# Row and token scales spread over partitions: from products with ones to a round trip through DRAM

## The reference, cut to what matters

```
def rms_norm(x, g):
    xf = x.astype(jnp.float32)
    y = xf * lax.rsqrt(jnp.mean(xf * xf, axis=-1, keepdims=True) + EPS)
    return (y * g.astype(jnp.float32)).astype(x.dtype)
...
        ple_gate = jax.nn.sigmoid(jnp.einsum('bsd,de->bse', rms_norm(x, norm_ple_g[i]), w_ple_gate[i]))
        x = x + ple_gate * jnp.einsum('bsq,qd->bsd', p[i], w_ple_proj[i])
    return rms_norm(x, norm_final_g)
...
    def step(carry, inp):
        C, n, m = carry
        C_l, n_l, am, gc = inp
        m_new = jnp.maximum(gc + m, am)
        sp = jnp.exp(gc + m - m_new)
        sl = jnp.exp(am - m_new)
        C_new = sp[..., None, None] * C + sl[..., None, None] * C_l
```

## Time and profile before

| What | Value |
|---|---|
| median of three runs | 1969.47 us |
| the profiled execution, as timed | 1970.42 us |
| its span in the profile | 1968.6 us |
| PE busy | 1884.6 us (96%) |
| VectorE busy | 729.1 us (37%) |
| ScalarE busy | 516.8 us (26%) |
| mean DMA rate over the span | 257 GB/s |
| mean granted TensorE clock | 0.989 |

### The profile page before, as it was taken

One profiled execution on the slowest core, in us unless ns is written; L12 is line 12 of the kernel. 1 busy time (PEld: TensorE's weight loads), 2 busy tenths in 40 slices (PEclk: granted clock), 3 DMA queues, 4 the chain that ended last, 5 costly groups with the idle time before them and its releaser, 6 DMA issues.

```text
span 1968.6 us, 20653 instructions
## 1 busy us (share of the span) xinstructions
PE 1884.6 (96%) x8719; PEld 1146.5 (58%) x8719; DVE 729.1 (37%) x1216; ACT 516.8 (26%) x836; POOL 58.6 (3%) x58
## 2 busy tenths in 40 slices
PE   8999999999999999999997999999889998999898
PEld 6788888888887888877874333333333332333332
DVE  7544444333356765886453111111111110111112
ACT  5444323222245343276622000000000000000002
POOL 1000000000014001000010000000000000000000
PEclk9999999999999999999998999999999999999999
DMA  5221322322323234212387999999999999999997
GB/s 190 86 86 65 118 96 97 97 97 96 107 95 107 75 112 161 75 65 78 141 328 292 430 432 434 430 432 433 433 432 434 430 433 433 431 433 433 431 429 294
DMA packets 50476, 506.89 MB, mean 257 GB/s; under 512 B 6544, under 2 KB 7568, under 8 KB 31696
## 3 DMA queue, kind: packets, MB, share of 16 engines
q1 hardware_dynamic: 48288, 502.22, 62.3%
q10 hardware_dynamic: 2096, 3.35, 0.5%
HBM read 501.23 MB, written 4.33 MB: 257 GB/s over the span
## 4 chain that ended last, share of the span: by engine, by line
PE 73%; DMA 23%; DVE 2%; ACT 2%; issue 1%; ACTq 0%; SPq 0%; DVEq 0%
PE ps L2133 40%; DMA ring_a<-in_experts_in 23%; PE ps L2484 10%; PE ps L2495 7%; PE ps L2068 4%; PE ps L2443 2%; PE ps L2467 1%; PE ps L2305 1%; PE ps L2530 1%; PE ps L2282 1%; PE ps L2506 0%; ACT hidT L1255 0%; PE ps L2183 0%; PE ps L2180 0%; PE ps L2186 0%
## 5 line engine op out<-in xcount | busy, mean ns | idle before, releaser
L2484 PE MATMUL ps<-ring_a,xe 128*64 128x512 f32 x1504 | 343.8, 610 | 41.9 <-DMA ring_a<-in_experts_in 41.1
L2484 PEld LDWEIGHTS ps<-ring_a,xe 128*64 128x64 f32 x1504 | 107.0, 140 | 272.8 <-issue 211.4
L1300 DVE TENSOR_TENSOR d_lo<-d_raw,d_hi 128x1024 fp32r<-128x1024 f32 x166 | 204.4, 1240 | 118.9 <-ACT d_hi L850 118.2
L2133 PE MATMUL ps<-n_hi,d_hi 128*128 128x512 f32 x448 | 176.0, 393 | 1.5 <-DVE d_lo L1300 0.8
L2133 PE MATMUL ps<-n_lo,d_hi 128*128 128x512 f32 x448 | 174.5, 389 | 0.0
L2133 PE MATMUL ps<-n_hi,d_lo 128*128 128x512 f32 x448 | 174.3, 389 | 0.0
L850 ACT ACTIVATE d_hi<-d_raw 128x1024 fp32r<-128x1024 f32 x166 | 170.8, 1049 | 8.6 <-DMA d_raw<-in_tiles_in 6.9
L1530 DVE TENSOR_TENSOR hid<-hid,ps 128x512 f32<-128x512 f32 x32 | 20.7, 684 | 409.1 <-PE ps L2484 382.7
L1976 DVE TENSOR_TENSOR acc<-acc,ps 128x1024 f32<-128x1024 f32 x56 | 64.6, 1215 | 244.5 <-PE ps L2467 244.5
L2495 PE MATMUL ps<-ring_a,hidT 128*64 128x512 f32 x648 | 145.9, 596 | 8.7 <-DMA ring_a<-in_experts_in 5.5
L2484 PE MATMUL ps<-ring_b,xe 128*64 128x512 f32 x464 | 103.1, 593 | 1.6 <-DMA ring_b<-in_experts_in 1.6
(11 more groups left out here) (499 smaller groups left out, 2710.6 us busy)
## 6 DMA issues: line engine op xcount, KB each, us to landing
ring_a<-in_experts_in SPq DMA_DIRECT2D x56, 4096.0 KB, 41.8
ring_b<-in_experts_in SPq DMA_DIRECT2D x28, 3072.0 KB, 42.7
d_raw<-in_tiles_in SPq DMA_DIRECT2D x166, 512.0 KB, 3.3
ring_a<-in_experts_in SPq DMA_DIRECT2D x31, 1024.0 KB, 12.4
ring_a<-in_experts_in SPq DMA_DIRECT2D x12, 2048.0 KB, 13.4
ring_b<-in_experts_in SPq DMA_DIRECT2D x5, 2048.0 KB, 13.2
ring_b<-in_experts_in SPq DMA_DIRECT2D x8, 1024.0 KB, 16.6
x_in<-in_xT_in SPq DMA_DIRECT2D x4, 512.0 KB, 6.7
```

The costliest lines, as they stand in the source:

```text
L1300: dve.tensor_tensor(d_lo[:, n % SLOTS, :, :], d_raw[:, n % SLOTS, :, :], d_hi[:, n % SLOTS, :, :].bitcast(F32), ALU.subtract).then_inc(t_l ...
L2133: mm = pe.matmul(bank, lt[:, n, gr.k0 + k, :], rt[:, k, :], start=k == 0 and m == 0, stop=k == gr.nk - 1 and m == 2)
L2484: mm = pe.matmul(ps[half * CAP:(half + 1) * CAP, 2 * m + q, :], xe[:, k, :], slot(e, n)[:, (2 * q + half) * S:(2 * q + half + 1) * S], sta ...
```

## The change

The four products, the three diagonals of 128 x 512, the one of 64 x 256, the three VectorE copies and the one ScalarE copy go away. In their place the 128 x 4 scales are stored in DRAM, element by element, and loaded back as a row to all partitions. The first two stores and loads stand in SP's queue in front of the load of a tile, and SP waits for the reciprocal and for its own store; VectorE waits for the load. The router's scale is stored together with dq's and loaded at out2 0. The chunk decays (64 x 4) go through ScalarE's queue, beside the row maxima.

```diff
+            def first_after(name, i):
+                return min(n for n in range(SLOTS, len(TILES)) if LAST[n - SLOTS] >= AT[name, i])
...
                     if STREAM[FIRST[n]].i == 0:
                         sp.wait_ge(do_lo.sem, do_lo.count("lo", NH - 1))
+                        sp.wait_ge(d_q.sem, d_q.count("root", NH - 1))
+                        sp.dma_start(rf[:, :], scale_store[1].rearrange("t p -> (t p)").partition_broadcast(P)).then_inc(s_rf, 16)
                     load_weights(STREAM[FIRST[n]].i, STREAM[FIRST[n]].i + 1)
+                if n == first_after("gate", 0):
+                    sp.wait_ge(pr_dve.sem, pr_dve.count("rstd"))
+                    sp.dma_start(scale_store[0].rearrange("t p -> p t"), sm[:, 52:56], allow_slow_non_contiguous=True).then_inc(s_scale, 16)
+                    sp.wait_ge(s_scale, 16)
+                    sp.dma_start(R[:, :], scale_store[0].rearrange("t p -> (t p)").partition_broadcast(P)).then_inc(s_R, 16)
+                elif n == first_after("dq", 0):
+                    sp.wait_ge(fn_dve.sem, fn_dve.count("rstd"))
+                    sp.dma_start(scale_store[1:3].rearrange("a t p -> p (a t)"), sm[:, 48:56], allow_slow_non_contiguous=True).then_inc(s_scale, 16)
+                    sp.wait_ge(s_scale, 32)
+                    sp.dma_start(R[:, :], scale_store[2].rearrange("t p -> (t p)").partition_broadcast(P)).then_inc(s_R, 16)
                 load1(n)
...
                 act.dma_start(rows_store[:, :], rown[:, :]).then_inc(s_nms, 16)
+                act.dma_start(carry_store[:, :], sm[0:64, 20:24]).then_inc(s_carry, 16)
...
-                act.wait_ge(r_pe.sem, r_pe.count("spb"))
-                r_act.done(act.activation(spb[:, :, :], ps[:, 6, 0:256], ACT.Copy), "spb")
...
                 elif (name, i) == ("mqk", 7):
                     convolved(7)
+                    act.wait_ge(s_carry, 16)
+                    act.dma_start(spb[:, :, :].rearrange("p r t -> p (r t)"),
+                                  carry_store.rearrange("r t -> (r t)").partition_broadcast(P)).then_inc(s_carried, 16)
...
                         link(pr_dve, dve.reciprocal(sm[:, 52:56], sm[:, 48:52]), "rstd")
-                        link(pr_dve, diagonal(dg, 52), "dg")
-                        dve.wait_ge(r_one.sem, r_one.count("R"))
-                        link(pr_dve, dve.tensor_copy(R[:, :], ps[:, 7, :]), "R")
+                        dve.wait_ge(s_R, 16)
...
-                        dve.wait_ge(f_one.sem, f_one.count("R"))
-                        link(fn_dve, dve.tensor_copy(R[:, :], ps[:, 3, :]), "R")
+                        dve.wait_ge(s_R, 32)
+                        dve.wait_ge(f_one.sem, f_one.count("gates"))
...
                         dve.wait_ge(s_x3, 16)
+                        dve.wait_ge(s_rf, 16)
...
-                elif (name, i) == ("ub", 0):
-                    link(t_dve, diagonal(dgf, 48), "dgf")
-                elif (name, i) == ("ub", 3):
-                    dve.wait_ge(t_pe.sem, t_pe.count("rf"))
-                    link(t_dve, dve.tensor_copy(rf[:, :], ps[:, 2, :]), "rf")
...
                 elif (name, i) == ("proj", 5):
-                    pe.wait_ge(pr_dve.sem, pr_dve.count("R"))
+                    pe.wait_ge(pr_act.sem, pr_act.count("root"))
...
-                pe.wait_ge(r_dve.sem, r_dve.count("spd"))
-                r_pe.done(pe.matmul(ps[:, 6, 0:256], ones[0:64, :], spd[:, :, :], start=True, stop=True), "spb")
...
-                    pe.wait_ge(pr_dve.sem, pr_dve.count("dg"))
-                    r_one.done(pe.matmul(ps[:, 7, :], ones[:, :], dg[:, :, :], start=True, stop=True), "R")
...
-                    pe.wait_ge(fn_dve.sem, fn_dve.count("dg"))
-                    read_done(pe, "proj", 7)
-                    f_one.done(pe.matmul(ps[:, 3, :], ones[:, :], dg[:, :, :], start=True, stop=True), "R")
-                elif (name, i) == ("ub", 1):
-                    pe.wait_ge(t_dve.sem, t_dve.count("dgf"))
-                    t_pe.done(pe.matmul(ps[:, 2, :], ones[:, :], dgf[:, :, :], start=True, stop=True), "rf")
```

More of the change, by code:

```diff
@@ L282, in kernel_program @@
 def kernel_program(nc, xT_in, pT_in, table, tri_in, gla_mask_in, rstm_in, negm_in, m01_in, dist_in, tiles_in,
-                   wgk_in, gkw_in, mgw_in, selg_in, diff_lam_2, w_router_2, experts_in, norm_f_g_2, x3_store, rows_store, out):
+                   wgk_in, gkw_in, mgw_in, selg_in, diff_lam_2, w_router_2, experts_in, norm_f_g_2, x3_store, rows_store, carry_store, scale_store, out):
     ctx = ExitStack()
@@ L527, in kernel_program @@
         p_dve = Steps(sem("p_dve"), ["lo0", "lo1"])
-        r_one = Steps(sem("ple_sum"), ["sum", "R"])
+        r_one = Steps(sem("ple_sum"), ["sum"])
         pr_act = Steps(sem("ple_root"), ["root"])
-        pr_dve = Steps(sem("ple_rstd"), ["rstd", "dg", "R"])
+        pr_dve = Steps(sem("ple_rstd"), ["rstd"])
         pl_dve = Steps(sem("ple_dve"), ["x", "lo"], 8)
@@ L533, in kernel_program @@
         pl_pool = Steps(sem("ple_pool"), [f"{a}{k}" for k in range(1, KD) for a in ("a", "b")])
-        f_one = Steps(sem("final_sum"), ["sum", "gates", "R"])
+        f_one = Steps(sem("final_sum"), ["sum", "gates"])
         fn_act = Steps(pr_act, ["root"])
-        fn_dve = Steps(pr_dve, ["ma", "mb", "v", "rstd", "dg", "R", "gates"])
+        fn_dve = Steps(pr_dve, ["ma", "mb", "v", "rstd", "gates"])
         n2_dve = Steps(h_dve, [f"{a}{k}" for ks in NORMED.values() for a in ("h", "lo") for k in ks])
@@ L543, in kernel_program @@
         s_nms = sem("row_maxima_stored")
+        s_carry = sem("chunk_decays_stored")
+        s_carried = sem("chunk_decays_in")
+        s_scale = sem("token_scales_stored")
+        s_R = sem("token_scales_in")
+        s_rf = sem("router_scales_in")
         s_nm = [sem(f"row_maxima_in{n}") for n in range(2)]
@@ L604, in kernel_program @@
         s_g = sem("gain_in")
-        t_pe = Steps(sem("route_pe"), ["rf", "partA", "partB", "logits", "x0", "x1", "x2", "affT", "x3", "thrT", "count"])
+        t_pe = Steps(sem("route_pe"), ["partA", "partB", "logits", "x0", "x1", "x2", "affT", "x3", "thrT", "count"])
         t_act = Steps(sem("route_act"), [f"sq{k}" for k in range(KD)] + ["root", "exp"] + [f"x{t}" for t in range(TT)]
                       + ["tri", "ones"])
-        t_dve = Steps(sem("route_dve"), ["dgf", "rf", "rwg", "part", "raw", "mx", "sub", "rstd", "lg", "sum", "rec", "aff", "affk"]
+        t_dve = Steps(sem("route_dve"), ["rwg", "part", "raw", "mx", "sub", "rstd", "lg", "sum", "rec", "aff", "affk"]
                       + [f"{a}{n}" for n in range(CAP // 8) for a in ("top", "rep")][:-1]
@@ L1539, in way @@
                 return t[0:32] if d == 0 else t[32:64, ::-1]
-            def diagonal(out, c):
-                return mul(out[:, :, :], ident[:, :].unsqueeze(1).to_broadcast([P, TT, P]),
-                           sm[:, c:c + TT].unsqueeze(2).to_broadcast([P, TT, P]))
             def gate_forget():
@@ L1624, in mlstm_states @@
                 if n == 0:
-                    dve.wait_ge(r_act.sem, r_act.count("spb"))
+                    dve.wait_ge(s_carried, 16)
+                    dve.wait_ge(r_act.sem, r_act.count("cols1"))
                     dve.wait_ge(mq_act.sem, mq_act.count("silu", 7))
@@ L2211, in row_columns @@
                 r_pe.done(mm, "cols")
[L2212 to L2213 removed]
             def keys_turned():
                 pe.wait_ge(mq_act.sem, mq_act.count("silu", 7))
[L2217 removed]
+                pe.wait_ge(r_act.sem, r_act.count("cols1"))
                 for c in range(TT):
@@ L2339, in chain @@
                     r_one.done(mm, "sum")
-                elif (name, i) == ("gate", 0):
-                    pe.wait_ge(pr_dve.sem, pr_dve.count("dg"))
-                    r_one.done(pe.matmul(ps[:, 7, :], ones[:, :], dg[:, :, :], start=True, stop=True), "R")
                 elif (name, i) == ("mg", 0):
```

16 lines of the change are left out of this document (5 added, 11 removed).

## The result

The changed kernel takes 1980.25 us (median of 4 runs, 1978.8 to 1984.17), the kernel before in the same series 1969.68 us (1969.24 to 1972.62): ratio 1.0051, 95% interval 1.0039 to 1.0063. The forecast was 1967.1 us with a range up to 1971.8. The profiled execution took 1978.8 us with a span of 1977.0, 8.4 us more than the one before.

What follows compares the result with a forecast made beforehand. TensorE's arrival at the first expert was taken to set the end. Savings 0.86 + 0.86 + 0.49 + 0.2 = 2.4 us gave 1969.47 - 2.4 = 1967.1 us, range 1965.5 to 1969.0, with rivals 1964.4 to 1971.8.

Steps and rivals of the forecast that it cites:

- What bounds the kernel: Experts' DMA stream sets the end; its start follows TensorE's arrival at the first expert, so moving that moves the end equally.
- Price of a round trip: Scale store and load at gate 0 and dq: store 2.8 and 3.3 us, load of one row 3.0 to 3.3.
- the sign of being wrong: Scale stores at gate 0 and dq: a landing beyond 5 us would make the forecast wrong.
- small writes are dear: Rival: each 4-byte write takes 100 ns or more, TensorE stalls at dk 2 and gate 0; 1971.5 us, 12%.
- My bound from above: dq store: eight times the nearest row's price, 128 ns per piece, 8.2 us more.
- Its second half: Load of `R` to 128 partitions after the scale store: 3.2 us, from a row of 3.0 to 3.3.
- Gate 0: `R` at 588.8, VectorE 0.7 us later against 3.0 us of slack at proj 6; full 0.86 us kept.
- dq 1: Round trip 6.6 us; nothing lost below 8.3, tightest customer dk 2 after dk 0's read; 0.86 us kept.
- Chunk decays: TensorE's 0.49 us goes and is kept; VectorE starts up to 0.8 us later but has 4.04 us idle.
- Router's scale: At out2 0: rf's load adds 0.45 us (bounds 0 and 1.0); 0.2 of 0.86 us kept.
- The saving: Four removed products on TensorE's chain: at most 0.86 + 0.86 + 0.49 + 0.86 = 3.07 us, 0.16% of the time.
- Range and chances: Whole kernel: 1965.5 to 1969.0 us, rivals 1964.4 to 1971.8; over 0.2% faster 14%, slower 8%, same 78%.

Runs made afterwards that it cites:

- both causes are mended: Changed kernel with 16-byte store pieces, order of tokens turned in GpSimd's additions, and rf's load behind out2 2's tile: 1968.11 us, ratio 0.9991.
- rf_alone: Kernel before with only the router's scale sent through DRAM, its load in front of out2's first tile: 1973.64 us, ratio 1.0016.
- strided_sums: Kernel before with only the products that sum the squares reading every fourth token instead of a run of 128: 1974.51 us, ratio 1.0024.
- pieces16_rf: Changed kernel with sums over every fourth token, 16-byte store pieces, and rf's load behind out2 2's tile: 1970.85 us, ratio 1.0002.
- gate_alone: Kernel before with only the gate's scale sent through DRAM: 1973.26 us, ratio 1.0019.
- rf_behind2: Second run of the changed kernel with rf's load behind out2 2's tile: 1980.13 us, ratio 1.0051.
- after_again: The changed kernel unchanged, measured again in a later series: 1981.84 us, ratio 1.0060.
- rf_behind: Changed kernel with rf's load issued behind the load of out2 2's tile instead of ahead of out2's first: 1980.46 us, ratio 1.0052.
- pieces16: Changed kernel with sums over every fourth token, so that scale stores write 16-byte pieces: 1973.97 us, ratio 1.0019.
- probe2: Kernel before with ten other added small stores in its first block, varying pitch, piece size and count: 1970.18 us.
- probe: Kernel before with ten added stores of constants in its first block, varying count, piece size and distance: 1970.66 us.
- probe3: Kernel before with seven added loads in its first block, one row to 128 partitions against 128 rows: 1970.52 us.

## Why the prediction was wrong

*What bounds the kernel.* Right: TensorE's arrival at the first expert sets the end. The first slot is reloaded 9.2 us later, and the span is 8.4 us longer.

*Price of a round trip.* This is the step that failed, by the size of a term. I put the dq store at 3.3 us and the gate's at 2.8; they took 8.4 and 8.1, beyond the 5 us that I had named as the sign of being wrong. The waits that came of it (at dq with a load that took 2.8 us more than I had) are 2.3 + 5.6 = 7.9 of the 12.6 us between my -2.4 and the +10.2 counted above; 3.4 are the clock, 1.3 out2. I carried over a price for small pieces from reads the earlier trace rows, and it priced the time on the engines, which is indeed short (the burst of 0.9 us), but not the completion. The kind of rival was right, its law was not: I let "small writes are dear" grow with the count, 100 ns for each of the 64 pieces of an engine, and got 1971.5 us. Measured, 128 closely packed pieces already cost 8.1 us and 1024 cost 11.6; with 16 bytes between their starts 128 cost 1.4. My bound from above, 8.2 us on top of the store, did hold the measured value, but I gave the range only the 100 ns case, and to the whole rival 12%. Even with the bound, 128 ns a piece, my sums would have given some 1974 us: the other terms were short as well. The Trainium skill (DMA: Bandwidth & Descriptors, Specifications) says that the engine does read-modify-write below 512 bytes. Taken as a price, this would make the pieces of 16 and 64 bytes dear too, and they landed in 1.4 us; whether it is behind the 8 us of the packed ones, no run here shows.

*Its second half,* the load of `R` at 3.2 us, took 3.7 us at the gate and 6.0 at dq, where SP issues tile loads right behind it. With the store gone from 8 to 2.3 us it took 4.1; why isn't shown.

*Gate 0.* The slack was right: `R` came at 593.39 in place of 588.8, 4.6 late; 2.3 us of slack were left; the wait was 2.3 us.

*dq 1.* The threshold of 8.3 us was nearly right: 14.4 us from the reciprocal's end at 642.57 to VectorE's read are 6.1 too many, TensorE waited 5.6. The customer was another one: the wait ended with the read of dq 3, for which dk 1 needs bank 1, and not with dk 0's. That read ended at 660.56 before, 1.9 us ahead of where dk 1 would start, so the threshold was 6.9 + 1.9 = 8.8 us, and 14.4 - 8.8 = 5.6.

*The clock* had no term at all. In the changed kernel it is 1.7 us behind the wait at dq and as much at out2 (29 matmuls in 8.0 busy us, where 37 would fit). That the waits bring it about is likely and not shown: the kernel before has such a stretch at 1045 us without one.

*Chunk decays.* Right: 0.5 us kept at the keys, in the changed kernel and alone.

*Router's scale.* Priced at +0.45 us with bounds 0 and 1.0 for the load in front of out2's first tile. I took 432 GB/s for one row read by all partitions; it moves at 155 to 200, so 256 KB take 1.5 us and not 0.6. ScalarE waited 2.4 us for a tile and TensorE 2.0. I had written that both lines were on time within 0.1 us; with that, an upper bound of 1.0 was too tight.

*The saving* of 3.07 us of TensorE fits what is left when both causes are mended: 1.9 us in the median (interval 0 to 3.3), and 1.2 more are lost to GpSimd by the mending itself.

*Range and chances.* 8% for slower by over 0.2%, and an upper end that took in none of the cases between 100 and 128 ns a piece, though I had no row of a small write.

## What to carry over

Before a small result goes through DRAM, look at how its pieces lie, not only at how many there are: 4-byte pieces side by side from many partitions cost 8 us to complete, the same bytes as 16-byte pieces 1.4 to 3.3. Where no row shows an operation, put the whole of its upper bound into the range, and give a wait of TensorE of some microseconds an upper bound with a slow stretch of 1.7 us behind it. A product with ones that costs 0.86 us on a full engine is cheap against a round trip that somebody waits for; it pays to go through DRAM only where the trip is shorter than the slack, as with the chunk decays, or with 16-byte pieces at dq (6.4 us against 8.8). And before two profiled executions are compared, look for a dip of the clock that only one of them has: here one in the kernel before was worth 1.1 us.

## What the runs showed of the hardware

- Stores of closely packed 4-byte pieces: 8.1 us for 128 and 12.1 for 2048, with the DMA engines idle for most of it; 8 bytes 3.2 to 3.6; 16 bytes apart 1.4. 16 pieces alone landed in 1.3, 32 in 3.0. Which unit works through them isn't shown.
- A tile load behind such a store on the same queue landed after 13.7 us in `rf_alone`; in the kernel before, the load of this place landed after 3.2.
- A stationary operand of TensorE with a stride of 16 bytes: weight load 329 ns instead of 192, product 372 instead of 250, and a granted clock of 0.86 and 0.80 in the two stretches of 5 us behind the start of 16 of them (`strided_sums`; 0.79 and 0.87 in `pieces16_rf`). GpSimd's addition with one operand read at that stride: 1708 ns instead of 1300.
- The clock behind a wait of TensorE: 1.00 after 2.3 us (changed kernel), 3.0 us (`gate_alone`) and 3.1 us (`rf_behind2`); after 3.4 us 0.66 for 10 us in `after_again`, but 0.79 and 0.87 in `rf_behind`; 0.86 from 670 to 680 us after 5.6 us, and 0.66 to 0.68 there after 6.1 to 6.3 us. At out2 it was 0.83 around a wait of 2.0 us in the changed kernel and 0.85 in `after_again`, but 1.00 around 2.0 us in `pieces16` and 1.9 in `rf_alone`. What tells these apart isn't shown.
- A dip without a wait: 0.66 from 1045 to 1050 us in the kernel before and, at the same place, in `probe2`, with TensorE busy all the time; 1.00 there in `probe` and `probe3`, which have the same instructions at this place.
